# Gated feed-forward up projections: both parts of x as one 512-column operand past the high weights, and the two halves of each bank added by VectorE

## The reference

```python
D_FF = ((8 * D_MODEL // 3 + 255) // 256) * 256      # 2816

def _rmsnorm(x, g):
    x32 = x.astype(jnp.float32)
    y = x32 * lax.rsqrt(jnp.mean(x32 * x32, axis=-1, keepdims=True) + EPS)
    return (y * g.astype(jnp.float32)).astype(x.dtype)

def _swiglu(h, w_in, w_out):
    gate, up = jnp.split(h @ w_in, 2, axis=-1)
    return (jax.nn.silu(gate) * up) @ w_out

    for li in range(DEPTH):                          # first block, 2 layers
        g = norm_gains[li]
        x = x + 0.5 * _swiglu(_rmsnorm(x, g[0]), ffn_w_in[li, 0], ffn_w_out[li, 0])
        ...
        x = x + 0.5 * _swiglu(_rmsnorm(x, g[2]), ffn_w_in[li, 1], ffn_w_out[li, 1])
        ...
```

## Time and profile before

| | |
|---|---|
| timed runs | 1827.59 us median (1805.72 to 1828.56) |
| profiled execution | span 1825.6 us; no other time is listed for it, the nearest timed run is 1827.59, 2.0 us more |
| TensorE busy | 1757.0 us, 96% |
| VectorE busy | 1191.0 us, 65% |
| ScalarE busy | 957.9 us, 52% |
| GpSimd busy | 351.8 us, 19% |
| TensorE's granted clock | 0.99 in the mean |
| HBM | 163 GB/s over the span |

### The profile page before, as it was taken

How to read it: one execution, slowest core, us unless ns; L and a number is a source line. 1 busy time by engine, 2 the same in 40 slices (tenths; PEclk the granted TensorE clock), 3 DMA queues, 4 the chain that set the end, 5 groups by cost and what they waited for, 6 DMA issues and landing times.

```text
span 1825.6 us, 36701 instructions
## 1 busy us (share of the span) xinstructions
PE 1757.0 (96%) x14498; PEld 1721.6 (94%) x14498; DVE 1191.0 (65%) x1765; ACT 957.9 (52%) x1100; POOL 351.8 (19%) x280
## 2 busy tenths in 40 slices
PE   7999989989999899999999999989899999989998
PEld 7999989989999899998998999988899999989998
DVE  6655589976565665556456555665487776567776
ACT  5444667775444754444345444465455455655553
POOL 2000500030004600026663000566400011020001
PEclk9999999999999999999999999999999999999999
DMA  6656323335555365543434555434245454345552
GB/s 217 209 184 243 132 96 116 116 116 186 201 187 190 111 224 190 201 144 133 138 138 148 187 188 185 173 120 154 97 162 206 165 192 139 116 162 184 185 205 92
DMA packets 45168, 298.25 MB, mean 163 GB/s; under 512 B 5024, under 2 KB 5408, under 8 KB 15920
## 3 DMA queue, kind: packets, MB, share of 16 engines
q1 hardware_dynamic: 45104, 297.38, 46.0%
HBM read 296.31 MB, written 1.05 MB: 163 GB/s over the span
## 4 chain that ended last, share of the span: by engine, by line
PE 82%; DVE 10%; ACT 4%; issue 3%; DMA 1%; POOL 0%; SPq 0%; DVEq 0%; ACTq 0%
PE wk L379 15%; PE wk L380 15%; PE wk L381 15%; PE acc L379 8%; PE acc L380 8%; PE acc L381 8%; DVE x_lo L457 1%; PE wk L391 1%; PE wk L390 1%; PE wk L389 1%; PE wk L1043 1%; DVE sumsq L690 1%; DVE x L422 1%; ACT w_hi L325 1%; DVE w_lo L351 1%
## 5 line engine op out<-in xcount | busy, mean ns | idle before, releaser
L325 ACT ACTIVATE w_hi<-raw 128x2048 fp32r<-128x2048 f32 (+5 forms) x300 | 533.3, 1787 | 406.6 <-PE wk L381 337.7
L380 PE MATMUL wk<-x_lo,w_hi 128*128 128x256 f32 x2560 | 718.3, 281 | 0.0
L379 PE MATMUL wk<-x_hi,w_hi 128*128 128x256 f32 x2208 | 627.4, 284 | 21.4 <-DVE x_lo L457 16.5
L2618 POOL TENSOR_TENSOR w_lo<-raw,w_hi 128x512 fp32r<-128x512 f32 (+1 forms) x274 | 351.0, 1315 | 1459.0 <-ACT w_hi L325 1458.9
L381 PE MATMUL wk<-x_hi,w_lo 128*128 128x256 f32 x2208 | 620.6, 281 | 0.0
L351 DVE TENSOR_TENSOR w_lo<-raw,w_hi 128x2048 fp32r<-128x2048 f32 (+2 forms) x218 | 484.1, 2222 | 169.0 <-ACT w_hi L325 168.8
L380 PEld LDWEIGHTS wk<-x_lo,w_hi 128*128 128x128 f32 x2560 | 484.3, 189 | 0.3
L379 PEld LDWEIGHTS wk<-x_hi,w_hi 128*128 128x128 f32 x2208 | 422.9, 192 | 27.6 <-DVE x_lo L457 18.8
L381 PEld LDWEIGHTS wk<-x_hi,w_lo 128*128 128x128 f32 x2208 | 419.5, 190 | 0.0
L379 PE MATMUL acc<-h_hi,w_hi 128*128 128x256 f32 x1376 | 391.3, 284 | 16.3 <-DVE h_lo L2207 4.7
L380 PE MATMUL acc<-h_lo,w_hi 128*128 128x256 f32 x1376 | 387.7, 282 | 0.0
(11 more groups left out here) (325 smaller groups left out, 2140.5 us busy)
## 6 DMA issues: line engine op xcount, KB each, us to landing
raw<-w_ffn_loop SPq DMA_DIRECT2D x120, 1024.0 KB, 4.8
raw<-w_conv_loop SPq DMA_DIRECT2D x60, 1024.0 KB, 4.8
raw<-w_mla_loop SPq DMA_DIRECT2D x18, 768.0 KB, 4.2
raw<-w_hgrn_loop SPq DMA_DIRECT2D x10, 896.0 KB, 4.5
raw<-w_ple_gate SPq DMA_DIRECT2D x8, 1024.0 KB, 4.7
raw<-w_odd_loop SPq DMA_DIRECT2D x10, 768.0 KB, 4.3
raw<-w_even_loop SPq DMA_DIRECT2D x6, 1024.0 KB, 4.8
raw<-w_odd_proj SPq DMA_DIRECT2D x6, 1024.0 KB, 4.8
```

Of the source, the lines that this page charges most:

```text
L325: nc.scalar.activation(w_hi[slot][:, 0:n], raw[slot][:, 0:n], ACT.Copy).then_inc(S("hi_ready"), 1)
L379: nc.tensor.matmul(dst, hi, a_hi, start=start, stop=False, skip_group_check=True)
L380: nc.tensor.matmul(dst, hi, a_lo, start=False, stop=False, skip_group_check=True)
L2618: last = nc.gpsimd.tensor_tensor(w_lo[slot][:, a:b], raw[slot][:, a:b], w_hi[slot][:, a:b].bitcast(F32), ALU.subtract)
```

## The change

x_hi and x_lo become the two halves of one tensor, x_both: for each of the 8 channel blocks 256 tokens of the high part and behind them 256 of the low part; likewise the second pair. In the four gated phases (not in the convolution's) a tile is now two matmuls (`wide_tile`): w_hi stands while the 512 columns of both parts stream past into a whole bank, then w_lo with the 256 columns of the high part, added to the bank's second half. The bank's halves still have to be added. So each half of a group takes two banks where it had half of each: gate banks 0 and 1, up banks 2 and 3 of wk. VectorE adds the halves with a TENSOR_REDUCE from PSUM into SBUF (ff_sum), tells TensorE with a new semaphore up_summed, and then multiplies by rstd from SBUF; w_lo of the first unit stands between the reduce and the multiply. The opening of ffn2 keeps the three matmuls and its banks, and its sums are copies. The norm's mean goes to bank 3 of acc in ffn0, ffn1 and ffn3, since wk has no free bank, and TensorE waits for ln_mean before it clears acc.

```diff
         x = sb("x", [P, KD, SEQ])
-        x_hi = sb("x_hi", [P, KD, SEQ], F32R)
-        x_lo = sb("x_lo", [P, KD, SEQ], F32R)
+        x_both = sb("x_both", [P, KD, 2, SEQ], F32R)
...
-        q_both = sb("q_both", [P, KD, SEQ], F32R)
-        x_lo_2 = sb("x_lo_2", [P, KD, SEQ], F32R)
+        x_both_2 = sb("x_both_2", [P, KD, 2, SEQ], F32R)
...
+        def parts(both):
+            return both[:, :, 0, :], both[:, :, 1, :]
+        x_hi, x_lo = parts(x_both)
+        x_hi_2, x_lo_2 = parts(x_both_2)
+        q_hi, q_lo = x_hi_2[:, 0:4, :], x_lo_2[:, 0:4, :]
...
+        in_pairs_from = [ph[1] for ph in phases if ph[0] == "ffn"]
+        def in_pairs(name, opening=True):
+            return name in in_pairs_from and not (opening and name in same_norm)
+        def x_pair(name, k):
+            both = x_both_2 if name in second_x else x_both
+            return both[:, k, :, :].rearrange("p h t -> p (h t)")
...
+        def wide_tile(bank, pair, start=False):
+            def go(hi, lo):
+                nc.tensor.matmul(bank, hi, pair, start=start, stop=False, skip_group_check=True)
+                return nc.tensor.matmul(bank[:, SEQ:2 * SEQ], lo, pair[:, 0:SEQ], start=False, stop=True, skip_group_check=True)
...
         def norm_bank(name):
-            return acc[:, 3, :] if name.startswith("ple") else wk[:, 3, :]
+            return acc[:, 3, :] if name in ple_index or in_pairs(name) else wk[:, 3, :]
...
                 for half in range(2):
-                    need(pe, "up_read", 2 * (n0 + j) - 1 + half)
+                    need(pe, "up_summed" if name in in_pairs_from else "up_read", 2 * (n0 + j) - 1 + half)
                     hs = []
                     for k in range(KD):
                         for n in range(2):
-                            bank = wk[:, half + 2 if opening and name in same_norm else half, :]
-                            hs.append(channel_tile(bank[:, n * SEQ:n * SEQ + SEQ], xs_hi[:, k, :], xs_lo[:, k, :],
-                                                   start=(k == 0 and n == 0)))
+                            if not in_pairs(name, opening):
+                                bank = half + 2 if opening and name in same_norm else half
+                                hs.append(channel_tile(wk[:, bank, n * SEQ:n * SEQ + SEQ], xs_hi[:, k, :], xs_lo[:, k, :],
+                                                       start=(k == 0 and n == 0)))
+                            else:
+                                hs.append(wide_tile(wk[:, 2 * half + n, :], x_pair(name, k), start=(k == 0)))
...
             up(first, 0, 0, opening=True)
+            if in_pairs(name):
+                pe.wait_ge(S("ln_mean"), 2 * norm_index[name] + 2)
             pe_clear_acc(pe, name).then_inc(S("acc_cleared"), 1)
...
+        ff_sum = [work[:, 4616 + 512 * q:5128 + 512 * q].rearrange("p (n t) -> p n t", n=2) for q in range(2)]
...
             def group(seg, i, j, ahead=()):
                 bank = banks[2:4] if seg is first and name in same_norm else banks[0:2]
+                def summed(half):
+                    if seg is first and name in same_norm:
+                        ins = nc.vector.tensor_copy(ff_sum[half], bank[half])
+                    else:
+                        pair = wk[:, 2 * half:2 * half + 2, :].rearrange("p n (h t) -> p n t h", h=2)
+                        ins = nc.vector.tensor_reduce(ff_sum[half], pair, AX.X, ALU.add)
+                    ins.then_inc(S("up_summed"), 1)
...
                 o = 2 if conv else 0
-                nc.vector.tensor_tensor(ff_gate[:, :, o:o + SEQ], bank[0], over_tokens(rstd[:, :], 2), ALU.mult).then_inc(S("up_read"), 1)
-                if 0 in ahead:
-                    dve_rest(v, loop, j, 0)
+                if name in in_pairs_from:
+                    summed(0)
+                    if 0 in ahead:
+                        dve_rest(v, loop, j, 0)
+                    v.wait_ge(S("up_summed"), 2 * (n0 + j) + 1)
+                    nc.vector.tensor_tensor(ff_gate[:, :, 0:SEQ], ff_sum[0], over_tokens(rstd[:, :], 2), ALU.mult).then_inc(S("up_read"), 1)
+                else:
+                    nc.vector.tensor_tensor(ff_gate[:, :, o:o + SEQ], bank[0], over_tokens(rstd[:, :], 2), ALU.mult).then_inc(S("up_read"), 1)
+                    if 0 in ahead:
+                        dve_rest(v, loop, j, 0)
...
-                nc.vector.tensor_tensor(ff_up[:, :, o:o + SEQ], bank[1], over_tokens(rstd[:, :], 2), ALU.mult).then_inc(S("up_read"), 1)
+                if name in in_pairs_from:
+                    summed(1)
+                    v.wait_ge(S("up_summed"), 2 * (n0 + j) + 2)
+                    nc.vector.tensor_tensor(ff_up[:, :, 0:SEQ], ff_sum[1], over_tokens(rstd[:, :], 2), ALU.mult).then_inc(S("up_read"), 1)
+                else:
+                    nc.vector.tensor_tensor(ff_up[:, :, o:o + SEQ], bank[1], over_tokens(rstd[:, :], 2), ALU.mult).then_inc(S("up_read"), 1)
```

More of the change, by code:

```diff
@@ L260, in build @@
         lat = tmp[:, 0:4, :]
-        q_hi, q_lo = q_both[:, 0:4, :], q_both[:, 4:8, :]
+        def parts(both):
[3 more added lines that the diff above has]
+        q_hi, q_lo = x_hi_2[:, 0:4, :], x_lo_2[:, 0:4, :]
         k_rope = sb("k_rope", [P, SEQ])
@@ L273, in build @@
         second_x = {ph[1] for ph in phases if ph[0] == "ple"} | set(same_norm)
-        x_hi_2 = q_both
         def x_of(name):
             return (x_hi_2, x_lo_2) if name in second_x else (x_hi, x_lo)
+        in_pairs_from = [ph[1] for ph in phases if ph[0] == "ffn"]
[4 more added lines that the diff above has]
+            return both[:, k, :, :].rearrange("p h t -> p (h t)")
         from_acc = {b[1] for a, b in zip(phases, phases[1:]) if a[0] == "ple"} | set(same_norm)
@@ L381, in go @@
                 return nc.tensor.matmul(dst, lo, a_hi, start=False, stop=stop, skip_group_check=True)
+            return go
+        def wide_tile(bank, pair, start=False):
+            def go(hi, lo):
+                nc.tensor.matmul(bank, hi, pair, start=start, stop=False, skip_group_check=True)
+                return nc.tensor.matmul(bank[:, SEQ:2 * SEQ], lo, pair[:, 0:SEQ], start=False, stop=True, skip_group_check=True)
             return go
```

## The result

| | median | lowest to highest | against before |
|---|---|---|---|
| before | 1822.17 us (18 runs) | 1805.72 to 1834.18 | |
| after | 1837.55 us (18 runs) | 1830.30 to 1844.21 | 1.0096, 95% interval 1.0072 to 1.0120 |

A forecast was written before the change was run, and what follows sets the result against it. The prediction took TensorE's matmuls by their spacing as the bound, VectorE hidden. Terms: -11.0 (merge) + 3.6 (ffn0's start) + 0.9 (openings) = -6.5 us, so span 1819.1, time 1821 us; range 1795 to 1838.

The forecast's parts named there:

- What bounds it: Gated feed-forward loops: time is the number of matmuls by their spacing; TensorE busy 96% of the span, VectorE 65%.
- The gain of the 512: Gated loops: a tile falls from 340.0 to 333.3 or from 353.3 to 342.2 ns, together 11.0 us gained.
- rival 1: Gated loops: two 256s cost a 512, at 232 ns; time 1833 us; chance 15%.
- The bound I gave for the tile above: Gated loops: a 512 at 232 ns makes a tile 345 or 350 ns, a loss of 5 or gain of 3.
- That a loop keeps its spacing through the change: Gated loops: ffn1 and ffn2 counted as 113 ns loops, ffn0 and ffn3 as 118 ns loops, also after the change.
- My sum: Whole kernel: -11.0 + 3.6 + 0.9 = -6.5 us; span 1819.1, time 1821.
- Rival 4: Whole loops: spacing falls otherwise, 1799 us if short throughout, 1834 if ffn1 and ffn2 get the long one; chance 17%.
- my last sentence: Whole kernel: sign is wrong if the spacing of matmuls the change doesn't touch moves with the new pattern.
- R: Gated loops: time of one VectorE reduce of 128x1024 from PSUM, taken as 2.0 us, with 1.2 kept below.
- Rival 3: Gated loops: VectorE becomes the bound, slower than before; about 1846 us at a 2.5 us reduce, 1883 at 3.0; chance 9%.
- The start of ffn0: ffn0's first turns: two reduces push VectorE's angles and w_lo, delaying TensorE; cost 3.6 us, 1.9 with a 1.2 us reduce.
- The openings: Behind the openings, the loops of ffn3 and ffn1 start later by the reduce; cost 0.4 + 0.5 us, ffn2 0.

The follow-up runs named there:

- The bf16 stretches of these runs: Programs running set matmul patterns on TensorE alone, computing nothing of the reference; in bf16, 256 columns every 109.2 ns and 512 every 215.8 ns.
- the kernel with the 64s: Kernel before plus one 64-column matmul of zeros per turn of each feed-forward loop, between the up projection's halves; span 1818.3 us, one run.
- that with the 512s: Kernel before plus one 512-column matmul of zeros per turn of each feed-forward loop, between the up projection's halves; span 1847.6 us, one run.

## Why the prediction was wrong

1. **What bounds it**: right. TensorE's matmuls by their spacing, VectorE hidden.
2. **The gain of the 512**: this step failed. I priced it with one fixed part, 220 or 224 ns, a tile at 333 or 342. The 512 stood at 235.5 in every gated loop. I had the row of 232 ns and named two 256s for a 512 as rival 1 (15%), but took the 225 ns row because it stood beside a long stretch. Neither was a stretch of pairs. Two 256s at the long spacing are 235.6, so rival 1 had the right name; but I priced it at 232. The bound I gave for the tile above, 345 or 350 ns, was too low as well: it measured 353.3.
3. **That a loop keeps its spacing through the change**: the second half of the same failure, and the larger one. My sum took ffn1 and ffn2 as 113 ns loops, because this one trace had them so. They are not: any loop can be either, and the 512 takes the short one away. ffn1 and ffn2 lost 6.4 and 6.6 us where I had each gain 2.1, and ffn0 and ffn3 gained nothing where I had 3.2 and 3.5. That is 11.0 + 13.0 = 24 us between my sum and the traced loops. A third of those 13.0 lies in the 48 matmuls of the down projection in each turn, which the change does not touch. Rival 4 (17%) had the effect, 1834 us with ffn1 and ffn2 long, and my last sentence named it as what would turn the sign; but I gave it to "the new order or the day", with the short end as near as the long. Its cause was in the diff.
4. **The sum on VectorE**: R was 1.22 us, my lower bound, not 2.0. The source in PSUM with its parts 1 KB apart costs no more than dense elements. "VectorE: DVE Perf Modes" of the Trainium skill says as much in "The perf-mode tier table" (one element a cycle), and the trace agrees with it here: 1024 elements in 1.22 us. I had let the strided rows outvote it.'s 2.01 us has the same count and step, but reads four parts out of SBUF, not two out of PSUM; which of the two differences matters no run here shows. Rival 3 (9%) was gone with that.
5. **The start of ffn0**: 3.6 us forecast, 1.9 if R were 1.2. TensorE's second turn began 1.5 us later, 1.8 counted from the clearing (at 26.1 us before, 25.8 after), which is the 1.9 of the smaller R. The lower clock behind that wait, which I had not counted, took 1.4 more. But before's trace has its own stretch at a granted clock of 0.50 in this phase, from 207.4 to 210.6 us, where after has 1.00, so that between the two clearings after has only 2.1 us more.
6. **The openings**: 0.9 us forecast, 0.1 found in ffn1, since R is 1.2.
7. The range, 1795 to 1838, held the median of 1837.55 at its very edge. That was luck: it reached so far up for rivals 1 and 4 taken singly, and what happened has a part of each, while my sum had even the sign wrong.

The profiled spans differ by 13.3 us: 13.0 more for ffn1 and ffn2, 2.1 more for ffn0's stretch, 4.5 less for conv0, which was short in after, and 3.7 more between the second and the third clearing of acc, where the granted clock was lower (0.51 from 235 to 249 us, 0.89 in before's trace); the rest is shorter stretches. Over the whole span the clock was 0.987 against 0.990, so one pair of traces does not price the change. The medians, 15 us apart, average over how before's loops fall, and over how the clock fell: its mean over after's 18 runs is 0.991, and over before's runs in the later comparisons 0.989 to 0.991.

"TensorE: Matmul & The Clock Gate" of the Trainium skill, section "Back-to-back issue gap", gives N/2.4 + 2.5 ns as the gap of a single matmul and about 131 ns for 512 columns in a stream. The bf16 stretches of these runs, which are streams with a weight load for each matmul, agree with the formula (109.2 and 215.8 ns) and not with the 131. The float32r ones agree with neither: 120.0 and 226.7 alone, 113.3 or 117.8 and 235.5 in the kernel. By that page's formula a merge saves 2.5 ns a tile; here it cost up to 13.3.

## What to carry to other kernels

Count a merge of matmuls by its measured spacing in the stream where it will stand, and not by a fixed part taken from another row: here one 512 among 256s cost what two 256s cost at the long spacing, and it took the short spacing away. When the same instructions show two rates in one trace, treat the rate as a state that a stall or a foreign matmul can switch, look at a second trace before giving a loop "its" rate, and ask whether the change touches what holds it. Moving the state the same way in both versions (here by a few narrow matmuls, which did it in part) makes a blurred comparison clearer, and may be worth more than the change. Check in the traces that the state did move, and what the granted clock was.

## What the hardware showed that I had not expected

- float32r matmuls of 256 columns held 113.3 or 117.8 ns over 1440 in a row; at a stall the spacing could change (in ffn0 of the kernel with the 64s from 113.3 to 117.8 at 45.23 us, in that with the 512s from 117.8 to 113.3 at 45.24 us). Three matmuls of a tile thus took 340.0 or 353.3 ns, 20.0 or 33.3 more than 768 columns at 2.4 GHz.
- A 512-column matmul turned short stretches of 256s long, in both loops where it met one. A 64-column one turned long ones short in eight loops, in four of them at the first go and in four at the second, and in two loops three of them in a row did nothing. It cost 0.113 us (28 ns to the next start, 200 to the one behind, in place of 113).
- VectorE summed 1024 PSUM elements with parts 1 KB apart in 1.22 us, while a sum of as many elements in SBUF took 2.01.
- After 2.8 us in which TensorE started nothing, it ran near 1.2 GHz for over 3 us. The same wait of 2.4 to 3.1 us in ffn0 stands in six traces with the changed layout: in four the granted clock was 0.50 behind it, in two it stayed at 1.00.
